# A two-layer encoder trunk on one core: when the gates are asked for, and how a stage's first two chunks share each block of the norm

## The reference

```python
h = modulate(rmsnorm(x, norm1_g[l]), sh1, sc1)      # (h * (1 + scale) + shift), from c @ w_ada
z = h @ w_in[l]                                     # input projection, 1536 columns
ya = conv_mixer(z[..., :512], z[..., 512:1024], ...)  # GLU, causal depthwise conv of 31 taps, LayerNorm, silu
yb = pool_mixer(z[..., 1024:], ...)                 # trailing means over 2/4/8/16 frames, linear map
x = x + g1 * (jnp.concatenate([ya, yb], axis=-1) @ w_out[l])
h = modulate(rmsnorm(x, norm2_g[l]), sh2, sc2)
x = x + g2 * peer(h, ...)
# peer: q = h @ w_q; scores against 2 x 128 keys for each of 8 heads; the best 16 of each half,
# the best 16 of their 256 sums: expert ids, gate = softmax(best)
# y = sum over the 128 picks m of gate_m * gelu(u_tab[id_m] . h) * v_tab[id_m]   (16384 experts)
```

## Time and profile before

| | |
|---|---|
| median of 3 runs | 3432.2 us (3431.86 to 3432.84) |
| the profiled execution | 3433.31 us |
| its span in the trace | 3431.1 us |
| PE busy | 3339.3 us, 97% of the span |
| DVE busy | 2409.4 us, 70% |
| ACT busy | 1141.8 us, 33% |
| POOL busy | 723.8 us, 21% |
| HBM traffic | 197 GB/s over the span |

### The profile page before, as it was taken

The page is one execution under the profiler, slowest core; times in us unless marked ns, Lnnn a source line. Parts: engine busy times, 40 slices in busy tenths (PEclk is TensorE's granted clock), DMA queues, the critical chain, the costliest instruction groups (busy, mean ns, idle before and its releaser), DMA issues.

```text
span 3431.1 us, 55308 instructions
## 1 busy us (share of the span) xinstructions
PE 3339.3 (97%) x16402; PEld 2819.8 (82%) x16402; DVE 2409.4 (70%) x6151; ACT 1141.8 (33%) x1606; POOL 723.8 (21%) x437
## 2 busy tenths in 40 slices
PE   6999999899999999999999999999999999999998
PEld 4568888788888999999975688888888889999997
DVE  7972999699993456666677249936999734566665
ACT  3233222244343333333342332223444333333332
POOL 0033454300000013333100334441000000233330
PEclk8989999999999999999999999999999999999999
DMA  6153766445455668888721224443545656788884
GB/s 243 51 215 103 252 231 216 135 170 221 179 211 206 218 218 286 286 280 284 243 92 43 72 89 144 145 142 136 223 178 210 226 195 204 259 280 283 280 286 142
DMA packets 316570, 675.88 MB, mean 197 GB/s; under 512 B 28864, under 2 KB 176704, under 8 KB 314304
## 3 DMA queue, kind: packets, MB, share of 16 engines
q1 hardware_dynamic: 253248, 478.81, 42.4%
q10 hardware_dynamic: 40704, 128.88, 9.5%
q0 software_dynamic: 22528, 67.19, 5.2%
HBM read 546.66 MB, written 127.93 MB: 197 GB/s over the span
## 4 chain that ended last, share of the span: by engine, by line
PE 83%; DVE 12%; issue 4%; ACT 1%; DMA 1%; DVEq 0%; SPq 0%; ACTq 0%
PE bank L480 26%; PE bank L604 24%; PE bank L484 13%; PE bank L608 12%; PE bank L587 3%; DVE scratch L1200 2%; DVE scratch L1085 1%; PE bank L405 1%; DVE h L1178 1%; DVE h L1181 1%; PE bank L425 1%; DVE z_pad L1229 1%; DVE z_pad L1227 1%; DVE h L1180 1%; DVE h L1177 1%
## 5 line engine op out<-in xcount | busy, mean ns | idle before, releaser
L480 PE MATMUL bank<-h_hi,w_hi 128*128 128x512 f32 x2528 | 1002.8, 397 | 13.7 <-ACT norm_tmp L757 10.9
L480 PE MATMUL bank<-h_lo,w_hi 128*128 128x512 f32 x2528 | 987.9, 391 | 0.0
L643 ACT ACTIVATE w_hi<-ring 128x1024 fp32r<-128x1024 f32 x584 | 614.6, 1052 | 1118.0 <-PE bank L484 1061.9
L604 PE MATMUL bank<-v_hi,w_hi 128*128 128x448 f32 x2032 | 742.1, 365 | 0.0
L604 PE MATMUL bank<-v_lo,w_hi 128*128 128x448 f32 x2032 | 742.1, 365 | 0.0
L484 PE MATMUL bank<-h_hi,w_lo 128*128 128x512 f32 x2528 | 624.3, 389 | 0.0
L864 POOL TENSOR_TENSOR w_lo<-ring,w_hi 128x1024 fp32r<-128x1024 f32 x164 | 423.8, 2585 | 856.7 <-ACT w_hi L643 856.7
L480 PEld LDWEIGHTS bank<-h_hi,w_hi 128*128 128x128 f32 x2528 | 476.4, 188 | 115.4 <-ACT w_hi L643 14.0
L480 PEld LDWEIGHTS bank<-h_lo,w_hi 128*128 128x128 f32 x2528 | 476.4, 188 | 98.8 <-issue 2.4
L484 PEld LDWEIGHTS bank<-h_hi,w_lo 128*128 128x128 f32 x2528 | 474.6, 188 | 98.5
L1278 DVE TENSOR_SCALAR h<-iota_b,keys 128x128 f16<-128x128 f16 x1792 | 480.3, 313 | 0.0
(11 more groups left out here) (169 smaller groups left out, 2480.4 us busy)
## 6 DMA issues: line engine op xcount, KB each, us to landing
ring<-u_t SPq DMA_DIRECT2D x256, 512.0 KB, 3.5
ring<-v_t SPq DMA_DIRECT2D x256, 512.0 KB, 6.0
ga_scratch<-norm_tmp ACTq DMA_DIRECT2D x256, 256.0 KB, 2.0
g_scratch<-scratch ACTq DMA_DIRECT2D x14, 4096.0 KB, 13.4
scratch<-ga_scratch SPq DMA_DIRECT2D x256, 224.0 KB, 4.1
scratch<-g_scratch SPq DMA_DIRECT2D x128, 448.0 KB, 4.7
scratch<-ada_t SPq DMA_DIRECT2D x76, 512.0 KB, 5.6
ring<-wq_t SPq DMA_DIRECT2D x32, 512.0 KB, 3.4
```

The lines of the kernel that those rows point to most:

```text
L480: pe.matmul(to, w_hi[:, b, k * P:(k + 1) * P], part_h[:, k, :], start=(k == 0 and part_h is h_hi), stop=False)
L604: pe.matmul(bank[:, k, 0:TD], w_hi[:, b, k * P:(k + 1) * P], part_w[:, b, 0:TD], start=(first and part_w is v_hi), stop=False)
L643: return act.activation(to, of, ACT.Copy)
```

## The change

Four edits. `RETRIEVING` goes from 52 to 56, and with it EARLY from 60 to 64: ACT waits for the retrieval, PE for the gates, and POOL hands the low halves to DVE, four chunks later; the 56 chunks with gate blocks begin four later. In `first_two` every block of `h_hi` is multiplied for chunk 0 and chunk 1 when it arrives, and the low products of both come behind. In `other_half` the same is done for the convolution's four blocks. Ahead of the first norm's scaling DVE makes the low half of chunk 0, which was behind it.

```diff
-    RETRIEVING = 13 * N_U // 32
+    RETRIEVING = 14 * N_U // 32
...
                 for n in range(2):
                     wait_hi(pe, l, 0, stage + n)
-                    for i, k in enumerate(order):
-                        if n == 0:
-                            pe.wait_ge(hi_ready_h, 3 * KC * l + h_base + (i + 1))
+                for i, k in enumerate(order):
+                    pe.wait_ge(hi_ready_h, 3 * KC * l + h_base + (i + 1))
+                    for n in range(2):
                         pe.matmul(bank[:, 2 + n, :], w_hi[:, n, k * P:(k + 1) * P], h_hi[:, k, :],
                                   start=(i == 0), stop=False)
+                for n in range(2):
                     wait_lo(pe, l, 0, stage + n)
...
+                for k in range(CONV):
+                    pe.wait_ge(hi_ready_h, 3 * KC * l + KC + CONV + (k + 1))
+                    for n in range(2):
+                        pe.matmul(bank[:, 2 + n, :], w_hi[:, n, k * P:(k + 1) * P], h_hi[:, k, :], start=False, stop=False)
                 for n in range(2):
-                    for k in range(CONV):
-                        if n == 0:
-                            pe.wait_ge(hi_ready_h, 3 * KC * l + KC + CONV + (k + 1))
-                        pe.matmul(bank[:, 2 + n, :], w_hi[:, n, k * P:(k + 1) * P], h_hi[:, k, :], start=False, stop=False)
                     for k in range(CONV):
                         pe.matmul(bank[:, 2 + n, :], w_lo[:, n, k * P:(k + 1) * P], h_hi[:, k, :], start=False, stop=False)
...
+                lo(0)
                 scale(ROOTS * l, coef[:, 0, :], scaled)
-                lo(0)
                 lo(1)
                 lo_h(2 * l, 0, 0)
```

## The result

The changed kernel took 3415.78 us (median of 5 runs, 3411.68 to 3416.74), against 3432.84 us before (5 runs, 3431.86 to 3435.6). The ratio is 0.9945, with a 95% interval of 0.9935 to 0.9956. The profiled execution took 3411.68 us, and its span is 3409.5 us, 21.6 us less than before.

A forecast was written before the change was run, and what follows sets the result against it. The prediction took the kernel to be a row of PE-paced stages, PE carrying 83% of the chain of waits. Gains of 16.1 us in layer 0 and 4.7 in layer 1, together 20.8, gave a forecast of 3412 us, range 3409 to 3416.

The forecast's parts named there:

- The stop at chunk 54: Layer 0's up chunks: later gates remove PE's 8.98 us stop and 2.60 us slow restart, 11.6 us; layer 1 gains nothing.
- The cover at chunk 58: Layer 0: the retrieval could end 12.8 us later before PE notices; POOL's low halves would take 4.2 us of it.
- The gate store: End of the up stage: last gate store, issued 21.8 us later, stays hidden with 2.8 us to spare; cost 0.
- The query stage: First two chunks, each layer: gap-free matmuls, 13 of them slow, take 13.5 us instead of 16.10; gain 2.6 us twice.
- The input stage of layer 1: PE begins 0.26 us later but takes 13.5 us to chunk 2; gain 1.4 us, bounds 0.6 and 2.2.
- The input stage of layer 0: Scaling begins 1.3 us later, yet chunk 2 comes sooner and the gain goes through; 0.9 us, bounds -0.3 and 1.3.
- The output stages: Chunk 1's products made between convolution blocks; gain 1.0 us in layer 0, 0.7 in layer 1, bounds 0.5 and 1.3 each.
- The sum: All terms together: 16.1 us in layer 0 and 4.7 us in layer 1, 20.8 us off the profiled execution.
- The first low half's place: Input stages: chunk 0's low half ahead of the scaling delays the scaling 1.3 us in layer 0; priced within those stages' gains.

The follow-up runs named there:

- e1: The kernel before with only RETRIEVING moved from 52 to 56 (the gates alone); 3422.78 us, ratio 0.9973.
- e2: The kernel before with only the new orders of first_two and other_half, RETRIEVING still 52, first low half behind the scaling; 3425.52 us, ratio 0.998.
- e6: The changed kernel with each round's up tiles asked for ahead of the modulation tiles in layer 0; 3422.52 us, ratio 0.9969.
- e4: The changed kernel with RETRIEVING at 60, the gates four chunks later again; 3425.2 us, ratio 0.9973.
- e3: The changed kernel with the first low half back behind the scaling; 3412.24 us, ratio 0.9942.
- e9: The kernel before with RETRIEVING at 48, the gates four chunks sooner; one run, 3452.36 us.
- e5: The changed kernel run again without any edit; 3415.99 us, ratio 0.9951.
- e7: The changed kernel with only the last round of up tiles asked for ahead of the last four modulation tiles in layer 0; 3411.09 us, ratio 0.9933.
- e8: The kernel of e7 with the first low half back behind the scaling; 3409.14 us, ratio 0.9929.

## Why the prediction was right, point by point

**The stop at chunk 54** was priced at 11.6 us. It gave 11.58 in the changed kernel (up chunks 49 to 55) and 11.57 alone in e1. The 8.98 us and the 2.60 us of the restart went together, and nothing came back at chunk 58. In layer 1 the move gave nothing, as predicted: PE is 21.6 us ahead of before at the start of the up stage and at its end.

**The cover at chunk 58** was given as 12.8 us for the retrieval. The 4.2 us that POOL's low halves would take from it were 4.4 (two steps, e2 against the changed kernel). DVE, which had come forward 4.4 us with everything else, so ended its retrieval at the old time. The 12.8 us held for PE where it was before; with PE 5.85 us further ahead, about 7 were left (650.7 - 3.6 - 639.9, an estimate from the rows). e6 measures the cover: its PE was 8.7 us ahead of before, so a retrieval ending at 653.9 would be 653.9 - (656.5 - 8.7 - 3.6) = 9.7 us too late, and the stop was 9.5.

**The gate store** was to land 2.8 us ahead of the first load back; it was 3.2. The place was right, but the price of missing it was not as I put it. I let SP's lateness go through to PE in full. e4 had the store 21.8 us later, and PE lost 1.3 and 2.0 us by it, since DVE takes the first results long after they are asked for (in the changed kernel at 1081.8, 16 us after 1065.54). The larger loss of e4 is the pace of a whole stage, which I had not foreseen.

**The query stage** was priced at 2.6 us twice, with 13 slow matmuls. It gave 2.59 and 2.47. **The input stage of layer 1** was priced at 1.4, with PE starting 0.26 us later. PE started 0.26 us later (17.43 - 17.17), took 1.77 us less, and reached chunk 2 with a gain of 1.51 (18.94 - 17.43). Over all starts of this kind, the eight of before and e1 last 15.5 us on average from the first matmul to chunk 2 (15.1 to 15.9), the twelve of the changed kernel, e2 and e3 13.4 (12.5 to 13.8).

**The input stage of layer 0** was priced at 0.9, and was 1.14 at chunk 2; but I wrote that the gain goes through, and it did not. DVE waited 2.29 us for a modulation tile behind it (1.64 before), and 0.5 us of the 1.14 were left when the output stage began. Then the sums and the first products of the output stage met the lower clock for longer, and at the first convolution block nothing was left (+0.02). The granted clock of PE in that stretch (windows of the changed kernel: start and end, us, busy times, PEclk, DMA), where before it was 0.86 in the first and 0.72 in the second:

```profile
150.00:162.00 12.00, 10.85 (x27) 6.45 (x27) 7.35 (x22) 5.19 (x7) 0.00 (x0) 0.78 0.00 0
165.00:177.00 12.00, 9.86 (x39) 7.11 (x40) 10.35 (x15) 4.88 (x8) 2.84 (x1) 1.00 0.40 139
```

**The output stages** were mis-sized. In layer 0 I took 1.0. From the first convolution block on, PE reached chunk 2 3.33 us sooner, far over my bound of 1.3: it had two matmuls to a block, and the clock stayed up there (1.00 in the second window), where I had left the 14 matmuls from 168.34 to 174.57 at the lower one but for the three that go. 1.5 us of it were lost again behind: DVE's sum of the modulation took 2.13 us beside POOL's low half (0.17 before), and x and the squares came late. The net is 1.8. In layer 1 I took 0.7. From the first convolution block to chunk 2 it gave 0.68, but 0.50 had been lost ahead of it, where PE met the lower clock (0.88 against 1.00 before), so 0.2 is left.

One pair of executions is a weak witness here. From the first convolution block to chunk 2 the old order (before, e1, e9; both layers) took 8.3 us once, at a granted clock of 1.00, and 9.7 to 10.9 us five times, at 0.68 to 0.82. The new order (the other eight traces) took 7.6 us twelve times, at 1.00, and 9.0 to 9.2 us four times, at 0.81. So the new order keeps the clock up more often, not always, and the single 8.3 us is layer 1 of the execution from which I priced it.

**The sum** was 20.8 from the profiled execution. The profiled execution after is 21.6 us faster, but it gets there with 1.6 at chunk 48 that no term of mine held: behind PE's other stop the clock stayed up, and chunk 48 took 5.56 us instead of 7.20. Without it the sum is 20.0. That it lies so near to 20.8 is partly luck, since the misses in the output stages and behind layer 0's input stage offset each other. The median fell by only 17.1 us in these runs (3432.84 to 3415.78). It lies 3.8 us above the forecast of 3412, just inside its range of 3409 to 3416. I took the one profiled execution as standing for all; three of these five and four of the five in e5 are some 4 us slower and have more time at the lower clock. The stop at chunk 48 may be behind it, as e7 took both the stop and the scatter away, but no trace of a slower execution was taken, so the cause of the 3.8 us stays open.

The first low half's place, which I priced inside the input stage, has no gain of its own that shows. Both times the version with it in its old place had the lower median (3412.24 against 3415.78 and 3415.99, 3409.14 against 3411.09), so it may even cost a little; the intervals overlap.

## What to carry to other kernels

A wait in the middle of an engine's program order should stand where the thing waited for is sure to be ready, and its price is the idle time plus the slow restart of TensorE; it is checked by putting the wait four chunks later and four chunks sooner (e1, e9). Work that arrives in blocks should be given all matmuls that need only that block, so that PE has no gaps while it is slow (13.4 us for a start instead of 15.5). Before moving a transfer ahead in an ordered queue, ask who stands behind it: e6 cured a stop of 2 us and made one of 9.5, e7 moved one round of the same transfers and kept both.

## What the runs showed of the hardware that was not expected

A down stage of 128 chunks ran at 4.96 us a chunk in one layer and at 4.86 in the other, in the same execution, at full granted clock and with no wait of PE (e4): 0.207 us between matmuls instead of 0.203. And a clock that comes back earlier or later makes the same start differ between executions: layer 0's query stage, with the new order, took 12.5 us from its first matmul to chunk 2 in e2 and 13.8 in e8, at a granted clock of 0.87 and 0.78. In layer 1's output stage the old order took 8.3 us before and 10.8 in e1. So the gain of an edit at one start, read from one pair of executions, says little; over the four starts it was 8.5 us (4 x 2.12).
